# Attention layer of a two-layer decoder step on one core: sample pairs and prompt heads in one written-out program

## The chip, the core and the metric

The kernel runs on one core of a Trainium2 chip. The core has five engines with an instruction queue each: TensorE (PE: matmuls and transposes into PSUM), VectorE (DVE), ScalarE (ACT), GpSimd (POOL) and SyncE (SP, which here issues DMA transfers). They run side by side and meet through semaphores only; each works through its queue in order, so that an instruction that waits holds up all that stands behind it on its engine. PSUM has eight banks of 128 partitions by 512 numbers of 32 bits.

The metric is the device time of one execution in microseconds (us), as the median of several runs.

## What is computed

One inference step of a decoder with two layers, for a prompt of 256 tokens and for 8 samples of 4 new tokens each (32 rows) with 256 cached positions. Layer 0 is a gated delta-rule mixer and a mixture of experts, layer 1 is differential attention and a mixture of experts. The change is in layer 1's attention:

```python
def diff_attention(q, k, v, q_pos, k_pos, lam):
    ...
    s = jnp.einsum('bqhcd,bkhcd->bhcqk', qblk, k).astype(F32)
    mask = k_pos[None, :] <= pblk[:, None]
    p = jax.nn.softmax(jnp.where(mask, s, -jnp.inf), axis=-1)
    a = p[:, :, 0] - lam * p[:, :, 1]
    return jnp.einsum('bhqk,bkhe->bqhe', a.astype(v.dtype), v)
...
def diff_mixer(xn, k_rows, v_rows, q_pos, k_pos, w_q, lam_p, subln, w_out, lam_init):
    q = (xn @ w_q).reshape(B, L, DIFF_HEADS, 2, DIFF_DH)
    q = rope(q, q_pos) * (DIFF_DH ** -0.5)
    ...
    o = diff_attention(q, k, v_rows, q_pos, k_pos, lam)
    o = rms_norm(o, subln) * (1.0 - lam_init)
    return o.reshape(B, L, D_MODEL).astype(xn.dtype) @ w_out
```

There are 8 heads of two halves of 64. Keys and values of the new tokens come from one projection (`w_kv`, 1024 to 2048) and are outputs too; those of the past lie in a cache of pages of 128 rows, two pages for each sample, found through `page_table`. All is in float32.

## The kernel before

The program is five phases that follow each other with a barrier between: `gdn_phase`, `moe_phase` (layer 0), `attn_phase`, `moe_phase` (layer 1), `final_phase`. Weights pass through nine slots in SBUF, `slots` 0 to 8, 2 MB each. An expert phase works in groups of two experts, six slots to a group (gate, up and down matrices of two experts), and its SyncE queue fills each slot again when it is free. `m["prefetch"]` fills slots for the phase that comes. In the attention phase slots 0 to 5 hold the projection weights first; then slots 0 and 1 (`flat[0]`) hold the cached keys `Kc` and values `Vc` of two samples, slot 2 the spread queries `QB`, slots 4 and 5 the output weights `w_out`. Slots 6 to 8 share memory with the phase's own tiles.

`attn_phase` writes out one queue for each engine. On TensorE the order is:

1. **Projections.** For each half of 512 columns: keys, values and queries of the two prompt tiles (8 matmuls a tile, L1618), then all three for the 32 sample rows in one bank (`few`, L1626). DVE rotates keys and queries by position (`rotate`, L1467 to L1472), ACT scales the values into `v_t`. After the second half PE waits for all rotations, and transposes the sample rows (L1635).
2. **Samples** (`samples(pair)`), a loop over four pairs of samples. PE turns the cached keys, 32 transposes in eight groups of four over the four banks `B[4]` to `B[7]` (L1655), which DVE and ACT copy into `XK` (L1499, L1369). Then come the scores (L1666), a softmax over DVE and ACT (L1503 to L1510, L1371) in which PE runs 12 filler matmuls (`keep_busy`, L1642), the turned weights (L1672 to L1674), the sum over values (L1684), and transposes of the result (L1690), which DVE copies into `oT` (L1525). After the loop the sample rows are normed: a sum by a matmul with ones (L1697), a root on ACT, a reciprocal and a product on DVE (L1538, L1539).
3. **Heads** (`heads(i, ...)`), four rounds of two prompt heads, u = 0 and 1. PE makes the scores (L1721), turns queries and keys of the next two heads (L1709, from slices that GpSimd cut out, L1331), and runs 16 fillers. DVE adds the mask and finds maxima (L1548 to L1551), ACT takes four exponentials a head (L1392), DVE makes the weights (L1556 to L1565), PE turns them (L1734), ACT copies (L1399), PE multiplies by the values (L1745 to L1747), ACT squares and copies (L1405, L1406).
4. **Output.** Root, reciprocal and scaling of the prompt rows (L1415, L1585, L1588), transposes (L1759), the output projection of the prompt rows (64 records, L1766) and of the sample rows (L1770), and adds to the residual.

P, the sample's scores, and Pu, the heads' scores, are one tile; so are the sample's and the heads' maxima and sums. SyncE loads all keys of a pair when the keys of the pair before are turned, and its values when the pair's values are used. The output weights and expert piece 3 are issued ahead of the second pair's keys:

```python
            sp.wait_ge(s["kv_made"], 14)
            sp.dma_start(w_out, m["w_out_b"][0].rearrange("(h p) n -> p h n", p=128)).then_inc(s["wout_in"], 16)
            m["prefetch"](sp, 1, (3,))
            with sp.Fori(1, PAIRS) as pair:
                cache(0, pair, True)
                cache(1, pair, True)
```

## Time and profile before

| | us |
|---|---|
| median of 3 runs | 1624.23 |
| lowest and highest | 1622.6, 1625.52 |
| the profiled execution | 1618.63 |
| its span, first to last instruction | 1616.8 |
| attention phase on PE, from 847 to the next phase's start at 1126.8 | 280 |
| expert phase of layer 1 and the final norm, from there to the end | 490 |

The profile is of one execution. An engine is busy while it runs an instruction; the time of a PE instruction is counted to its modelled end, so that neighbours overlap. "Clock" is the share of TensorE's full speed (2.4 GHz) that was granted; 0.50 is 1.2 GHz. Each time in the trace is from the start of the span.

### The profile page before, as it was taken

The page shows a single profiled execution, that of the slowest core. Times are in us where ns is not written, and L with a number is a line of the kernel's source. Part 1 is how long each engine was busy: PE and PEld are TensorE (multiplying, and loading weights), DVE is VectorE, ACT ScalarE, POOL GpSimd, SP SyncE. Part 2 cuts the span into 40 slices and gives each one's busy share as a digit, 9 for nine tenths or more (in the row PEclk, how much of TensorE's full clock was granted, in tenths as well). Part 3 has the DMA queues.
Part 4 walks back from the last instruction along what each step waited for, and adds up shares of the span by engine and source line. Part 5 has one row for each costly group of instructions (what it writes and reads, how often), then busy time and mean ns, then how long its engine had stood idle before and what let it go on. Part 6 is the DMA issues. An engine that isn't in the chain of part 4 may idle for free. (4 is left out here: it accounts for less than half of the span.)

```text
span 1616.8 us, 21249 instructions
## 1 busy us (share of the span) xinstructions
PE 1514.0 (94%) x7887; PEld 772.9 (48%) x7887; DVE 641.2 (40%) x1656; ACT 299.2 (19%) x755; POOL 83.1 (5%) x143
## 2 busy tenths in 40 slices
PE   9999999999999999989989987869999999999986
PEld 8787877666333333333334444564633333333332
DVE  2656564545324242322333233551523333332324
ACT  2524243213101010000011011361210001010001
POOL 0101010101000000000000000100000000000000
PEclk9999999999999999999999989989999999999998
DMA  6432321639999999999993257504799999999994
GB/s 218 129 109 70 111 70 69 235 110 357 425 426 426 426 426 427 427 426 427 426 392 155 104 189 286 212 1 190 307 425 426 426 426 426 427 426 428 425 425 150
DMA packets 121838, 484.52 MB, mean 300 GB/s; under 512 B 18314, under 2 KB 53038, under 8 KB 73634
## 3 DMA queue, kind: packets, MB, share of 16 engines
q1 hardware_dynamic: 117442, 479.05, 73.6%
q0 software_dynamic: 4320, 4.42, 0.8%
q8 instruction: 53, 0.87, 0.2%
q14 instruction: 23, 0.19, 0.0%
HBM read 483.77 MB, written 10.97 MB: 306 GB/s over the span
## 5 line engine op out<-in xcount | busy, mean ns | idle before, releaser
L2360 PE MATMUL moe_ps_gate<-slots,moe_xrT 128*64 128x512 f32 x1024 | 229.0, 596 | 19.9 <-DMA slots<-in_w_gate_e_dram 19.9
L2360 PE MATMUL moe_ps_up<-slots,moe_xrT 128*64 128x512 f32 x1024 | 226.8, 595 | 0.0
L2388 PE MATMUL moe_ps_y<-slots,router_inputs 128*64 128x512 f32 x960 | 212.6, 595 | 0.0
L2240 DVE TENSOR_TENSOR resid<-resid,moe_ps_x 128x512 f32<-128x512 f32 x60 | 41.3, 688 | 265.2 <-PE moe_ps_x L2404 265.2
L2360 PEld LDWEIGHTS moe_ps_gate<-slots,moe_xrT 128*64 128x64 f32 x1024 | 73.6, 137 | 149.0 <-issue 148.0
L2360 PEld LDWEIGHTS moe_ps_up<-slots,moe_xrT 128*64 128x64 f32 x1024 | 71.3, 137 | 150.8 <-issue 138.7
L907 PE MATMUL gdn_bank<-gdn_xT,slots 128*128 128x288 f32 x512 | 133.0, 409 | 0.7 <-ACT slots L455 0.7
L2388 PEld LDWEIGHTS moe_ps_y<-slots,router_inputs 128*64 128x64 f32 x960 | 66.4, 137 | 124.8 <-issue 124.6
L2031 ACT ACTIVATE moe_xrT<-moe_ps_x,router_inputs 128x128 f32<-128x128 f32 x128 | 36.6, 369 | 379.5 <-PE moe_ps_x L2348 363.9
L907 PEld LDWEIGHTS gdn_bank<-gdn_xT,slots 128*128 128x128 f32 x512 | 93.9, 190 | 24.8 <-issue 1.8
L2209 DVE TENSOR_TENSOR router_inputs<-router_inputs,moe_ps_up 128x512 f32<-128x512 f32 x32 | 22.0, 689 | 195.3 <-PE moe_ps_up L2360 195.3
L2037 ACT ACTIVATE router_inputs<-moe_ps_gate 128x512 f32<-128x512 f32 x32 | 19.1, 598 | 233.3 <-PE moe_ps_gate L2360 233.3
L2404 PE MATMUL moe_ps_x<-moe_y_sb,router_inputs 128*128 128x512 f32 x120 | 59.5, 618 | 0.0
L1995 POOL DMA_INDIRECT moe_xrT<-xn_rows,moe_rows_in x30 | 31.0, 1032 | 526.4 <-PE moe_ps_x L2348 524.5
L2047 ACT COPY moe_y_sb<-moe_ps_y 128x512 f32<-128x512 f32 x32 | 18.8, 587 | 193.4 <-PE moe_ps_y L2388 176.5
L2232 DVE COPY moe_y_sb<-moe_ps_y 128x512 f32<-128x512 f32 x30 | 20.7, 692 | 81.3 <-PE moe_ps_y L2388 81.3
L2224 DVE TENSOR_SCALAR moe_place<-consts,moe_lpos,moe_gcur 128x128 f32<-128x128 f32 x192 | 52.1, 345 | 1.2
L2244 DVE TENSOR_TENSOR resid<-resid,moe_ps_up 32x256 f32<-32x256 f32 x112 | 46.2, 413 | 2.6
L1618 PE MATMUL at_bank<-slots,at_XK 128*128 128x512 f32 x96 | 41.7, 594 | 0.0
L1618 PE MATMUL at_pair<-slots,at_XK 128*128 128x512 f32 x96 | 41.5, 592 | 0.0
L665 DVE SCALAR_TENSOR_TENSOR slots<-slots,gdn_cw 128x312 f32<-128x312 f32 x72 | 39.2, 545 | 2.5
L2404 PEld LDWEIGHTS moe_ps_x<-moe_y_sb,router_inputs 128*128 128x128 f32 x120 | 20.3, 189 | 38.7 <-issue 38.7
(508 smaller groups left out, 1909.9 us busy)
## 6 DMA issues: line engine op xcount, KB each, us to landing
slots<-in_w_gate_e_dram SPq DMA_DIRECT2D x128, 1024.0 KB, 26.1
slots<-in_w_up_e_dram SPq DMA_DIRECT2D x128, 1024.0 KB, 26.5
slots<-in_w_down_e_dram SPq DMA_DIRECT2D x128, 1024.0 KB, 26.4
slots<-in_w_in_a_dram SPq DMA_DIRECT2D x16, 1024.0 KB, 5.5
slots<-in_w_kv_dram SPq DMA_DIRECT2D x4, 2048.0 KB, 17.1
slots<-in_cache_k_dram SPq DMA_DIRECT2D x16, 512.0 KB, 5.0
slots<-in_cache_v_dram SPq DMA_DIRECT2D x16, 512.0 KB, 5.5
slots<-in_state_delta_dram SPq DMA_DIRECT2D x8, 512.0 KB, 7.3
```

Of the source, the lines that this page charges most:

```text
L665: ins = V.scalar_tensor_tensor(acc[:, a, j, 0:ACC_COLS], src, cw[:, a, j, tap:tap + 1], acc[:, a, j, 0:ACC_COLS], ALU.mult, ALU.add)
L907: last = T.matmul(PB[i % 2][:, 0:T_ALL], w4[:, j, k, 128 * a:128 * a + 128], xT[:, k, :], start=(k == 0), stop=(k == KT - 1))
L1618: last = T.matmul(bank[:, :], XK[:, 0 if j < 2 else 1, k, at[t]], wslot[3 * half + j][:, k, :], start=(k == 0), stop=(k == KT - 1))
L1995: pool.indirect_dma_start(xg, None, xn_dram[:, :], bass.IndirectOffsetOnAxis(rows_in[:, :], 0), bounds_check=T_ALL - 1, oob_is_err=False). ...
L2031: last = A.activation(xgT[:, k, :], ps_x[:, 1, k - 4, :], ACT.Copy, scale=norm_T[:, k:k + 1])
L2209: V.tensor_tensor(hid, hid, ps_up[:], ALU.mult).then_inc(s["hidden"], 1)
L2224: last = V.tensor_scalar(place[:, k, t, :], m["lanes"][:, :], where[:, k, t:t + 1], gcur[:, k, t:t + 1], ALU.is_equal, ALU.mult)
L2240: V.tensor_tensor(half, half, banks[i][:, :], ALU.add).then_inc(s["summed"], 1)
L2244: V.tensor_tensor(part, part, banks[i][32 * q:32 * q + 32, 0:256], ALU.add).then_inc(s["summed"], 1)
L2360: last = T.matmul(ps[64 * e:64 * e + 64, :], xgT[:, k, 64 * e:64 * e + 64], slots[:, slot[2 * n + e], 512 * k:512 * k + 512], start=(k == ...
L2388: last = T.matmul(ps_y[64 * e:64 * e + 64, h, :], hidT[:, k, 64 * e:64 * e + 64], slots[:, slot[4 + e], 1024 * k + 512 * h:1024 * k + 512 ...
L2404: last = T.matmul(banks[i][:, :], selT[:, at[t]], y_sb[:, 512 * h:512 * h + 512], start=True, stop=True)
```

## The change

All of it is in `attn_phase`; the other phases are the same.

- Steps 2 and 3 become one program of four steps, written out without loops. Step i does sample pair i and heads 2i and 2i + 1, and turns keys for pair i + 1 and queries and keys for the next two heads in between.
- PSUM: turned keys have two banks (`turned_keys`, B[4] and B[5]) and not four, one copied by DVE and one by ACT. All small products of a pair share `S_bank` (B[6]), the sums over values of the pair and of both heads share `V_bank` (B[7]). Heads use the bank pairs `BB[u]` throughout.
- The sample's scores, weights, maxima and sums get tiles of their own (`sP`, `saT`, `smx`, `ssm`).
- Heads are transposed straight from `q_t` and `k_t`, sample scores read `QB` straight; GpSimd's copies go.
- Projections of the second half run in the order keys, sample rows, queries, (transposes of the sample rows), values.
- Keys are loaded a sample at a time, each when its place has been turned. The first loads of the second pair stand ahead of the output weights, and expert piece 3 stands behind all cache loads.
- Fillers: 8 and 8 in the last step, none in the others.
- The norm of the sample rows comes behind the last step, and their output projection ahead of the prompt rows' transposes.

The core of the diff, on PE and SyncE:

```diff
-            kbanks, vbanks, qbanks, few = (B[5], B[6]), (B[7], B[0]), (B[1], B[2]), B[3]
+            kbanks, vbanks, qbanks, few = (B[5], B[6]), (B[7], B[2]), (B[1], B[0]), B[3]
+            turned_keys, S_bank, V_bank = (B[4], B[5]), B[6], B[7]
+            out_banks = (B[5], B[7], B[6], B[0])
...
+            keys(0, 0)
+            keys(0, 1)
+            values(0)
+            sp.wait_ge(s["rotated"], 6)
+            rows_out(0)
+            for b in range(2):
+                sp.wait_ge(s["KT_made"], 4 * b + 4)
+                keys(1, b)
+            sp.wait_ge(s["kv_kept"], 6)
+            rows_out(1)
             sp.wait_ge(s["kv_made"], 14)
             sp.dma_start(w_out, m["w_out_b"][0].rearrange("(h p) n -> p h n", p=128)).then_inc(s["wout_in"], 16)
+            for pair in range(1, STEPS):
+                if pair < STEPS - 1:
+                    sp.wait_ge(s["KT_made"], 8 * pair + 4)
+                    keys(pair + 1, 0)
+                sp.wait_ge(s["od_made"], pair)
+                values(pair)
+                if pair < STEPS - 1:
+                    sp.wait_ge(s["KT_made"], 8 * pair + 8)
+                    keys(pair + 1, 1)
             m["prefetch"](sp, 1, (3,))
-            with sp.Fori(1, PAIRS) as pair:
-                cache(0, pair, True)
-                cache(1, pair, True)
...
+            for j in range(3):
+                project(0, j)
+            project_samples(0)
+            project(1, 0)
+            project_samples(1)
+            project(1, 2)
+            pe.wait_ge(s["rotated"], 6)
+            pe.wait_ge(s["q_rotated"], 4)
...
+            project(1, 1)
...
+            for i in range(STEPS):
+                more = i < STEPS - 1
+                sample_scores(i)
+                for u in range(2):
+                    scores(i, u)
+                if more:
+                    for j in range(2):
+                        turn_keys(i + 1, 0, j)
+                else:
+                    keep_busy(B[5], 0, 8)
+                sample_turned(i)
+                if more:
+                    for j in range(2, 4):
+                        turn_keys(i + 1, 0, j)
+                    for u in range(2):
+                        turn(i + 1, u)
+                else:
+                    keep_busy(B[5], 0, 8)
+                sample_values(i)
+                for u in range(2):
+                    weights_turned(i, u)
+                if more:
+                    for j in range(2):
+                        turn_keys(i + 1, 1, j)
+                sample_out(i)
+                if more:
+                    for j in range(2, 4):
+                        turn_keys(i + 1, 1, j)
+                for u in range(2):
+                    head_out(i, u)
+
             pe.wait_ge(s["od_sq"], 1)
-            T.matmul(B[0][:, 0:256], ones[:, :], rot2[:, 0:256], start=True, stop=True).then_inc(s["od_sum"], 1)
...
+            T.matmul(S_bank[:, 0:256], ones[:, :], rot2[:, 0:256], start=True, stop=True).then_inc(s["od_sum"], 1)
+            pe.wait_ge(s["od_done"], 1)
+            pe.wait_ge(s["wout_in"], 16)
```

The same steps in VectorE's queue:

```diff
+            for i in range(STEPS):
+                more = i < STEPS - 1
+                sample_scores(i)
+                scores(i, 0)
+                sample_weights(i)
+                if more:
+                    keys_kept(i + 1, 0, 0)
+                scores(i, 1)
+                sample_turned(i)
+                if more:
+                    keys_kept(i + 1, 0, 2)
                 for u in range(2):
                     weights(i, u)
+                sample_rows(i)
+                if more:
+                    keys_kept(i + 1, 1, 0)
+                sample_out(i)
+                if more:
+                    keys_kept(i + 1, 1, 2)
```

PE's queue in the second round of the sample loop, before. The names are tiles: `slots` holds the cached keys, `at_P` the scores and `at_aT` the weights.

```order
L1655 MATMUL at_bank<-consts,slots 128x128 x16
L1652 REGISTER_ALU
L1655 MATMUL at_bank<-consts,slots 128x128 x16
L1658 REGISTER_ALU
L1661 REGISTER_ALU
L1666 MATMUL at_pair<-at_XK,at_QBs 32x288 x16
L1642 MATMUL at_pair<-consts 128x128 x12
L1672 MATMUL at_pair<-consts,at_P 128x64
L1673 MATMUL at_pair<-consts,at_P 128x64
L1674 MATMUL at_pair<-consts,at_P 32x64
L1675 ISA
L1684 MATMUL at_pair<-slots,at_aT 32x512 x8
```

The same engine from the sample scores of a step to its sample values, now:

```order
L1708 MATMUL at_bank<-at_XK,slots 32x288 x16
L1760 MATMUL at_pair<-at_qkT 128x128 x2
L1760 MATMUL at_pair<-at_qkT 128x256 x2
L1760 MATMUL at_pair<-at_qkT 128x128 x2
L1760 MATMUL at_pair<-at_qkT 128x256 x2
L1692 MATMUL at_bank<-consts,slots 128x128 x8
L1715 MATMUL at_bank<-consts,at_sP 128x64
L1716 MATMUL at_bank<-consts,at_sP 128x64
L1717 MATMUL at_bank<-consts,at_sP 32x64
L1692 MATMUL at_bank<-consts,slots 128x128 x8
L1748 MATMUL at_pair<-consts,at_q 128x128 x2
L1748 MATMUL at_pair<-consts,at_k 128x128 x2
```

The 12 fillers (L1642) between scores and turned weights have given way to the scores of two heads and eight key transposes, which stood in one block of 32 ahead of the scores.

VectorE's queue before, in a round of the heads:

```order
L1548 TENSOR_TENSOR at_P<-at_pair,consts 128x768
L1549 TENSOR_REDUCE at_mx<-at_P 128x2
L1550 TENSOR_REDUCE at_mx<-at_P 128x2
L1551 TENSOR_SCALAR at_mx<-at_mx 128x4
L1548 TENSOR_TENSOR at_P<-at_pair,consts 128x768
L1549 TENSOR_REDUCE at_mx<-at_P 128x2
```

And now, from the scores of head 0 to those of head 1 of a step:

```order
L1565 TENSOR_TENSOR at_P<-at_pair,consts 128x768
L1566 TENSOR_REDUCE at_mx<-at_P 128x2
L1567 TENSOR_REDUCE at_mx<-at_P 128x2
L1568 TENSOR_SCALAR at_mx<-at_mx 128x4
L1531 RECIPROCAL at_ssm<-at_ssm 128x1
L1532 TENSOR_TENSOR at_ssm<-at_ssm,at_coef 128x1
L1533 TENSOR_SCALAR at_sP<-at_sP,at_ssm 128x288
L1516 COPY at_XK<-at_bank 128x2x256
L1565 TENSOR_TENSOR at_P<-at_pair,consts 128x768
```

The sample's weights and a copy of turned keys stand between the two heads' scores.

## Rows read from the trace of the kernel before

**Rows 1.** Stages: stretch, length, busy us (instructions), clock, DMA, GB/s.

```profile
847.00:946.90 99.90, 99.79 (x312) 42.86 (x312) 29.39 (x82) 9.97 (x15) 1.81 (x1) 1.00 0.30 112
946.90:963.10 16.20, 9.26 (x48) 8.33 (x48) 8.68 (x32) 3.95 (x8) 0.61 (x1) 0.58 0.81 288
963.10:1031.40 68.30, 51.39 (x456) 33.39 (x456) 22.70 (x69) 10.85 (x22) 3.26 (x7) 0.95 0.74 271
1031.40:1083.80 52.40, 40.75 (x298) 35.46 (x298) 33.56 (x90) 31.08 (x126) 4.33 (x12) 0.89 0.21 88
1083.80:1126.80 43.00, 35.00 (x145) 17.36 (x145) 7.02 (x11) 5.21 (x11) 0.01 (x1) 0.90 0.36 147
1126.80:1616.80 490.00, 465.57 (x2234) 183.47 (x2234) 174.17 (x432) 60.44 (x134) 21.67 (x34) 0.98 0.94 392
```

**Rows 2.** Timeline of PE, projections to scores: start, us, what, idle before.

```profile
951.53 1.06 PE L1635 MATMUL at_bank<-consts,at_q 32*128 32x32 f32 x8 [4.63 <-DVE at_q L1472]
...
963.16 2.15 PE L1666 MATMUL at_pair<-at_XK,at_QBs 128*32 128x288 f32 x32 [0.68 <-ACT at_XK L1369]
```

**Rows 3.** Timeline of PE, second and third sample pair.

```profile
979.30 3.67 PE L1655 MATMUL at_bank<-consts,slots 128*128 128x128 f32 x16 [5.31 <-DMA slots<-in_cache_k_dram]
...
1000.08 1.97 PE L1655 MATMUL at_bank<-consts,slots 128*128 128x128 f32 x16 [0.68 <-ACT at_XK L1369]
...
1002.80 2.15 PE L1666 MATMUL at_pair<-at_XK,at_QBs 128*32 128x288 f32 x32 [0.75 <-ACT at_XK L1369]
...
1009.37 1.92 PE L1684 MATMUL at_pair<-slots,at_aT 128*32 128x512 f32 x16 [0.50 <-DVE at_aT L1515]
...
1013.18 0.65 PE L1690 MATMUL at_pair<-consts,at_rot 128*128 128x128 f32 x4 [0.90 <-DVE at_rot L1517]
```

**Rows 4.** DVE: timeline of a pair and a heads round; last, lines by form.

```profile
1005.01 0.42 DVE L1503 COPY at_P<-at_pair 128x256 f32<-128x256 f32 x1 [2.67 <-PE at_pair L1666]
...
1007.16 0.17 DVE L1508 RECIPROCAL at_sm<-at_sm 128x1 f32<-128x1 f32 x1 [0.70 <-ACT at_P L1371]
...
1007.56 0.37 DVE L1510 TENSOR_SCALAR at_P<-at_P,at_sm 128x288 f32<-128x288 f32 x1
...
1062.27 0.96 DVE L1548 TENSOR_TENSOR at_P<-at_pair,consts 128x768 f32<-128x768 f32 x1
...
1064.42 0.18 DVE L1556 RECIPROCAL at_sm<-at_sm 128x4 f32<-128x4 f32 x1
...
L1499 DVE COPY at_XK<-at_bank 128x512 f32<-128x512 f32 x10 | 6.7, 690 | 4.7 <-PE at_bank L1655 4.7
```

**Rows 5.** Timeline of PE, head rounds.

```profile
1066.38 0.55 PE L1734 MATMUL at_bank<-consts,at_P 128*128 128x128 f32 x3 [1.21 <-DVE at_P L1565]
...
1081.37 0.39 PE L1745 MATMUL at_bank<-at_v,at_aT 128*128 128x128 f32 x2
```

**Rows 6.** Timeline of PE in the output part; last, of DVE.

```profile
1087.96 3.67 PE L1759 MATMUL at_pair<-consts,at_q 128*128 128x128 f32 x16 [4.21 <-DVE at_q L1588]
...
1092.41 27.73 PE L1766 MATMUL at_bank<-slots,at_oT 128*128 128x512 f32 x64 [0.78 <-ACT at_oT L1419]
...
1120.08 3.66 PE L1770 MATMUL at_pair<-slots,at_oT 128*32 128x256 f32 x64
...
1033.18 1.75 DVE L1538 RECIPROCAL at_rot<-at_rot 128x256 f32<-128x256 f32 x1 [1.82 <-ACT at_rot L1377]
```

**Rows 7.** Stretches as in rows 1, shorter.

```profile
979.70:983.00 3.30, 3.27 (x16) 2.86 (x14) 1.38 (x2) 0.59 (x1) 0.00 (x0) 0.50 0.90 369
995.30:1011.70 16.40, 13.37 (x130) 8.83 (x122) 6.25 (x18) 2.98 (x6) 0.61 (x1) 1.00 0.72 256
1041.00:1044.50 3.50, 1.17 (x9) 0.93 (x10) 2.57 (x10) 2.36 (x10) 0.00 (x0) 1.00 0.33 138
1044.80:1047.50 2.70, 2.70 (x16) 2.48 (x16) 0.00 (x0) 1.71 (x11) 0.00 (x0) 0.50 0.00 0
1108.50:1126.70 18.20, 15.24 (x92) 6.82 (x90) 3.03 (x6) 0.00 (x0) 0.00 (x0) 0.99 0.02 10
```

478 lines of the change are left out of this document (227 added, 251 removed).

## The prediction

> **What bounds the kernel now.** I read the table of stages first, then the row of TensorE (PE) through the attention layer, then what VectorE (DVE) and ScalarE (ACT) do while PE waits, then the granted clock. Stages [rows 1]: the second expert layer, from 1126.8 us to the end, keeps the DMA engines busy 94% of the time, since it streams all expert weights. The attention layer ahead of it is not bound by DMA. Its projections (847 to 946.9 us) are solid PE work. Then come 16.2 us of getting started (PE busy 9.3), 68.3 us in which the four sample pairs run one after another, 52.4 us in which the eight prompt heads run two at a time, and 43.0 us of output projection. In the two middle stages PE, DVE and ACT take turns: in the heads stage DVE has 33.6 and ACT 31.1 us of work in 52.4 us, and part of what PE does there is filler. So these 121 us are a chain of hand-offs. What shortens it moves the start of the expert layer, and that layer's first six-slot group is already loaded or loaded at its start, so the rest should move with it one to one: the stream of weights restarts when the layer starts.
>
> **The change, part by part.** I walk the new program against PE's row.
>
> *From projections to the first sample scores.* Before, PE ends projecting at 946.9 us, stands 4.63 us for the last rotation, transposes the sample rows (1.06 us and as much again for the keys), and begins the first sample scores at 963.16 us [rows 2]: 16.3 us. Now the sample rows of the second half are projected ahead of the query and value tiles, so their rotation and the transposes (about 2 us) lie in the projections. What is left behind the last projection is 8 groups of four key transposes and two head turns. Sixteen key transposes took 1.97 us at full clock [rows 3], so a group is 0.5 us. A head turn, four transposes of the same shape, is 0.5 too. That is 5 us. Since turned keys now have two PSUM banks and not four, a group waits for the copy of the group two ahead of it: a copy takes 0.69 us on DVE [rows 4], the group 0.5, so three or four times PE stands some 0.35 us. Sum 6.3 us, with the 2 us moved inward 8.4. Gain 16.3 - 8.4 = 7.9 us. It counts on the clock: before, the stage had 0.58 of full speed after the 4.63 us wait [rows 1, 2], and that wait is gone.
>
> *One step (a pair and two heads).* I set t = 0 at the start of the sample scores. They take 2.1 us on PE [rows 3]; the scores of the two heads and two key groups follow on PE to 4.7. DVE then has the long chain. Sample scores to maximum: from 1005.01 to the reciprocal at 1007.16, less the exponential of 0.70 between them, 1.45 us, so to 3.5. Scores of head 0: 1062.27 to 1064.42, 2.15, to 5.7. Sample weights: from 1007.16 to the end of the scaling at 1007.93, 0.8, to 6.5. Key copy 0.7, to 7.2. Scores of head 1 to 9.4. Copies of the turned sample weights 0.5 (PE's wait for them at 1009.37 [rows 3]), to 9.9. Key copy to 10.6. Weights of heads 0 and 1, 1.96 each (1064.42 to the PE row it releases at 1066.38), to 14.5 [all rows 4, 5]. PE then has the turn of the second head's weights 0.55 [rows 5], two key groups 1.0, the sample output transposes 0.65 [rows 3], two key groups 1.0, and the head outputs: six matmuls, whose first takes 0.39 with its drain [rows 5] and whose others follow at the fillers' pace or a little faster, 1.3. The next scores begin at **19.1 us**. The sample value matmuls (some 3 us on PE from 1009.37 [rows 3]) and the sample's exponential and the ACT copies lie beside that chain. PE waits about 1.9 us once (4.7 to 6.6, for the sample weights) and 1.2 us once (for head 1's weights), elsewhere under half a microsecond. The last step has no keys to turn: DVE ends its weights at 13.1, PE its head outputs at 15.8. Four steps: 3 x 19.05 + 15.8 = 73.0 us. Before, from 963.16 to the end of the last head output at 1083.7, 120.6 us. Gain 47.6 us. In it is the 5.31 us that PE stood for the keys of the second pair [rows 3], which were queued behind the output weights (4 MB) and an expert piece (2 MB). Now both halves of these keys are queued ahead of the output weights, and the expert piece behind all cache loads. What is late next are the third pair's keys and the second pair's values, behind those 4 MB; by the walk they are wanted some 4 us after they should land. If they are late, it costs at most the same 5.3 us once.
>
> *The tail.* Before, PE stands 4.21 us after the last head output (root, reciprocal, scaling), transposes for 3.67 us at half clock, and starts the output projection at 1092.41 [rows 6]. Now the sample rows' norm, which used to lie between pairs and heads, comes here, and PE waits for it first: its reciprocal alone is 1.75 us [rows 6], so PE stands about 6.0 us. The sample rows' projection (3.66 us [rows 6]) then runs ahead of the transposes; after such a wait it starts at 1.2 GHz as the transposes did, so I take 5.5. It hides the scaling, and the transposes run at full clock, 2.0. The large projection starts 13.6 us after the last head output, against 8.7 before, and is no longer followed by the 3.66 us. Between the end of PE's last matmuls (1120.08 + 3.66) and the layer's start at 1126.8 lie 3.1 us with four adds; now it is one, and I take 1 us for the other three. Sum: +4.9 - 3.7 - 1 = +0.2, call it **0.3 us lost**.
>
> *What costs nothing.* GpSimd's copies of queries and of head slices go; they lay beside PE work. Loops written out: their branches and register sums go, some tenths of a microsecond in each round, which I don't count. Expert pieces 3, 0, 2, 1 and the router inputs are issued before the tail, more than 40 us ahead of the layer's start. Pieces 6 to 8 were issued at the start of the output projection, and at 1108.5 DMA stood still [rows 7]: 16 us, and now they have 28. If that cover were gone, the expert layer would start with a wait for them.
>
> *The clock.* The walk is at full clock. The filler matmuls are gone, except for 16 in the last step. In the heads stage PE ran 1.17 us of 3.5 (1041 to 1044.5) and the clock was then 0.50 for 2.7 us; such falls came in three of four rounds and before the transposes. In the sample rounds, with waits under 1 us, it stayed at 1.00 [rows 7]. A step's 1.9 us wait lies between the two. From below the cost is 0; from above, a fall in each step and one of them twice as long, 2.7 us or more of half speed, so 1.4 to 2 us each, up to 9 in all. I take one short fall per step, 1.4 x 4 = 5.5 us, since one wait and its neighbours leave PE busier than that heads row.
>
> A rule bears on this: the Trainium skill, TensorE: Matmul & The Clock Gate, Part 4: PE-mode transpose, says that transposes do not count as work for the clock. By it the new filling of the waits, key and head transposes, would be worth nothing to the clock. Rows 7 speak against it: between 979.7 and 983.0 PE ran key transposes alone at 0.50, and that was enough: the rounds behind it ran at 1.00.
>
> **Sum.** 7.9 + 47.6 - 0.3 - 5.5 = 49.7 us. The profiled execution was 1618.6 us (span 1616.8 and 1.8 around it), 5.6 under the median of 1624.2. So 1569 for its like, and **1574 us** for the median.
>
> **Rivals.**
> 1. *The interleaving holds less than walked.* DVE and ACT are in order, so one late hand-off delays the other stream too. For it: DVE carries 15 us of each 19, with two chains through ACT. Against it: each queue is written in the order in which I find the results. Before, a pair and a heads round took 16.4 + 12.4 = 28.8 us. If half of what I claim of it is lost, a step is 24 us, 4 x 4.9 = 20 us back: 1594; a quarter gives 1584.
> 2. *The clock stays at 1.2 GHz through all steps*, by the transpose rule or because no filler is left. PE has some 15.5 us of work in a step: 13.4 in a pair's 16.4 us [rows 7], less 12 fillers of 0.24 us (as two key transposes [rows 3]), and 5 for two heads (1.1 and 1.3 [rows 5], 1.0 for the turns, 1.6 for the scores, estimated from the same shapes). At half speed that is 31 us, so 12 us more in three steps and 10 in the last: 46 us, in place of 5.5: 1615. The rule cited above would give this time.
> 3. *Slower: it stays there through the tail as well.* The output projection is 27.7 us of solid matmuls [rows 6] and doubles, with 4 for the rest: 1615 + 31 = 1646. It decides when more than 110 us run at half speed, as each such microsecond costs half of one. Against it: before, 3.67 us of transposes at half clock were enough, and the 64 output matmuls behind them took 0.43 us each from the first on [rows 6].
> 4. *The change does not bring the end forward*, since the expert layer gives the gain back. For it: its DMA share of 0.94. Against it: DMA stood at about zero from 1108.5 to 1126.7 [rows 7], so it isn't the stream that was late when the layer began. Time 1620 to 1625.
>
> **Numbers.** Forecast (1564 to 1581, with the bounds 0 and 9 us for the clock and the 5.3 of late loads) 0.70; rival 1, 1581 to 1594, 0.18; rival 2 0.04; rival 3 0.03; rival 4 0.05. The range 1562 to 1590 takes in the forecast and most of rival 1. A measurement here can tell about 0.2% (3 us) from no change. Faster by more: 0.70 + 0.18 + 0.04 = 0.92; same 0.04; slower 0.04 (rival 3 and the far side of rival 4).
>
> **What the new profile would show.** Right: no PE wait over 1 us between the last projection and the first sample scores, scores of the pairs 19 to 21 us apart, no wait on the key or value cache, a PE wait near 6 us before the sample rows' projection, and the same 490 us from the expert layer's start to the end. Wrong if pairs lie 24 us or more apart (then see which engine PE waits for), if the clock row shows 0.5 over whole steps, or if the expert layer takes longer than 490 us.

## The result and the profile after

The changed kernel takes 1559.74 us (median of 4 runs, 1558.21 to 1562.42), against 1623.6 for the kernel before in the same comparison (4 runs, 1622.6 to 1625.52). The ratio is 0.9615, 95% interval 0.9589 to 0.9641: 64 us less. The forecast was 1574 us in a range of 1562 to 1590. The direction was right, and the time lies 14 us below the forecast and 2 us below the range.

The profiled execution of the changed kernel took 1558.21 us, its span 1556.4. First its stages, to be laid beside [rows 1] (stretch, length, then busy us and instructions of PE, PEld, DVE, ACT, POOL, the granted clock, DMA share, GB/s):

```profile
846.70:949.40 102.70, 102.70 (x328) 45.31 (x329) 35.68 (x110) 10.86 (x18) 1.81 (x1) 0.98 0.32 120
949.40:955.70 6.30, 5.13 (x43) 4.28 (x42) 2.77 (x4) 4.14 (x9) 0.00 (x0) 1.00 0.24 69
955.70:1025.10 69.40, 63.16 (x552) 43.52 (x553) 50.94 (x157) 35.54 (x134) 0.00 (x0) 0.93 0.80 290
1025.10:1068.10 43.00, 35.55 (x149) 16.54 (x148) 9.17 (x14) 6.06 (x17) 0.05 (x1) 0.96 0.70 288
1068.10:1556.40 488.30, 466.86 (x2234) 183.37 (x2234) 174.23 (x432) 60.40 (x134) 21.62 (x34) 0.98 0.94 393
```

The sample pairs and the prompt heads took 68.3 and 52.4 us one after the other. Together they now take 69.4, with PE busy 91% of it. That is 51 of the 60 us by which the profiled span is shorter. PE's row through these four steps:

```profile
955.69 2.15 PE L1708 MATMUL at_bank<-at_XK,slots 128*32 128x288 f32 x32 [0.72 <-DVE at_XK L1516]
...
962.04 0.43 PE L1715 MATMUL at_bank<-consts,at_sP 128*128 128x64 f32 x2 [1.66 <-DVE at_sP L1533]
...
973.76 2.15 PE L1708 MATMUL at_bank<-at_XK,slots 128*32 128x288 f32 x32
...
979.41 1.62 PE L1692 MATMUL at_bank<-consts,slots 128*128 128x128 f32 x8 [1.99 <-DMA slots<-in_cache_k_dram]
...
991.87 2.15 PE L1708 MATMUL at_bank<-at_XK,slots 128*32 128x288 f32 x32
...
1005.82 0.88 PE L1768 MATMUL at_pair<-consts,at_P 128*128 128x128 f32 x6
...
1010.35 2.15 PE L1708 MATMUL at_bank<-at_XK,slots 128*32 128x288 f32 x32
...
1025.13 0.60 PE L1824 MATMUL at_bank<-at_rot,consts 128*128 128x256 f32 x2
...
1031.16 5.25 PE L1829 MATMUL at_bank<-slots,at_oT 128*32 128x256 f32 x64 [5.43 <-DVE at_oT L1612]
```

The rows of 2.15 us are the sample scores, where a step begins. The first begins at 955.69 (955.3 by the walk, at 963.16 in [rows 2]), the next three 18.07, 18.11 and 18.48 us apart, and the last step is 14.78 long. The walk had 19.05 and 15.8. In each of the first three steps PE stands once for 1.6 to 2.0 us (in the second it is for the third pair's keys), and in the last for 0.62. The last row is the samples' projection, behind the longest wait of the tail.

The granted clock fell to 0.50 once in each of the first three steps, for about 3 us. The prediction had charged one such fall in each of the four. One of these falls, and the one behind the tail's wait:

```profile
1000.50:1003.50 3.00, 3.00 (x17) 1.88 (x19) 2.86 (x13) 2.68 (x11) 0.00 (x0) 0.50 0.01 3
1031.20:1034.60 3.40, 3.40 (x36) 1.64 (x40) 2.43 (x3) 0.00 (x0) 0.00 (x0) 0.53 1.01 429
```

And DVE's row in the third step. It has no gap from 994.09 to 1005.36:

```profile
994.09 0.42 DVE L1523 COPY at_sP<-at_bank 128x256 f32<-128x256 f32 x1 [3.19 <-PE at_bank L1708]
994.43 0.18 DVE L1524 TENSOR_TENSOR at_sP<-at_bank,consts 128x32 f32<-128x32 f32 x1
...
995.21 0.96 DVE L1565 TENSOR_TENSOR at_P<-at_pair,consts 128x768 f32<-128x768 f32 x1
...
997.99 0.68 DVE L1516 COPY at_XK<-at_bank 128x512 f32<-128x512 f32 x1
998.59 0.95 DVE L1565 TENSOR_TENSOR at_P<-at_pair,consts 128x768 f32<-128x768 f32 x1
...
1001.63 0.15 DVE L1573 RECIPROCAL at_sm<-at_sm 128x4 f32<-128x4 f32 x1
...
1003.45 0.17 DVE L1573 RECIPROCAL at_sm<-at_sm 128x4 f32<-128x4 f32 x1
...
1004.61 0.75 DVE L1582 SCALAR_TENSOR_TENSOR at_P<-at_P,at_sm 128x128 f32<-128x128 f32 x2
1005.96 0.69 DVE L1546 COPY at_rot<-at_bank 128x512 f32<-128x512 f32 x1 [0.60 <-PE at_bank L1731]
```

PE turns the heads' weights from 1005.82 on. DVE had them ready at 1005.36 (1004.61 and 0.75). So two chains end this step within half a microsecond of each other: DVE's, and PE's own work, which had the clock fall in it. That is the question for the experiments.

### The profile page after: what moved, and what is told of

Same layout as the page of the kernel before. It is cut to its first block and busy times, and to the rows that moved or that the text cites. A ratio compares the mean times of both kernels' runs of the same rounds, so it can differ in the third digit from the quotient of the medians.

```text
span 1556.4 us, 20606 instructions
## 1 busy us (share of the span) xinstructions
PE 1485.6 (95%) x7695; PEld 744.9 (48%) x7695; DVE 638.5 (41%) x1656; ACT 294.5 (19%) x753; POOL 74.6 (5%) x123
```

## Experiments: what the parts are worth

Each kernel was compared with the kernel before on the same chip. The chips differ by a few microseconds, so between comparisons the ratios are set side by side, and small effects are read from the traces. "Steps" is the time from the first sample scores to the last head output: 69.4 us in the changed kernel.

**The loops written out, nothing else** (nine loops of this kind):

```
-            with sp.Fori(1, PAIRS) as pair:
+            for pair in range(1, PAIRS):
```

> The kernel before, with nothing changed but that the attention stages' nine register loops are written out for every step. Theory (order of the work is what pays): the written-out form alone gives 0 to 2 us of the 64, 1622 to 1624 us. Rival (the loops' registers, branches and semaphore arithmetic held the engines up): 10 us or more, under 1614 us.

Measured: 1618.43 us against 1619.38, ratio 0.9998 (0.9982 to 1.0013). Writing out the program is worth nothing by itself, within the 2 to 3 us that this comparison can tell. It is only what makes another order possible.

**The new layout, the old order of the work.** The four pairs run first, then the heads:

(PE's part; the other engines' orders follow it, SyncE loads a pair's values ahead of the next pair's keys, and twelve and sixteen fillers stand in PE's waits as before.)

```
+            for i in range(STEPS):
+                sample_scores(i)
+                keep_busy(B[0], 0, 12)
+                sample_turned(i)
+                sample_values(i)
+                sample_out(i)
+                if i < STEPS - 1:
+                    for b in range(2):
+                        for j in range(4):
+                            turn_keys(i + 1, b, j)
+            for u in range(2):
+                turn(0, u)
             for i in range(STEPS):
                 more = i < STEPS - 1
-                sample_scores(i)
                 for u in range(2):
                     scores(i, u)
...
```

> The changed kernel with its PSUM layout, its projection order and its written-out program, but the four sample pairs one after the other first and the prompt heads behind them, as in the kernel before. Theory (interleaving fills the waits of one chain with the work of the other): the 47.6 us of the step-by-step part come back, 1600 to 1612 us. Rival (the new layout of PSUM and of the key loads carries a good part by itself): under 1590 us.

Measured: 1613.39 us, ratio 0.9969 (0.9951 to 0.9987). The two stretches of its trace, and its one long wait for a load:

```profile
953.30:1016.70 63.40, 49.80 (x458) 32.73 (x459) 21.33 (x64) 9.53 (x20) 0.00 (x0) 1.00 0.86 313
1016.70:1069.40 52.70, 38.85 (x296) 34.73 (x295) 31.57 (x93) 27.84 (x118) 0.00 (x0) 0.90 0.29 118
...
978.72 1.92 PE L1721 MATMUL at_bank<-slots,at_saT 128*32 128x512 f32 x16 [2.72 <-DMA slots<-in_cache_v_dram]
```

They sum to 116.1 us, against 120.6 before and 69.4 when interleaved. By the traces the interleaving is worth 46.7 us and the layout, with its key loads, 4.5; up to 2.7 of the 46.7 is this wait for the second pair's values, which neither the kernel before nor the changed one has. The first theory holds. The median lies 1 us above the bound expected. By the ratios the interleaving would be worth more, some 55 us: the profiled execution (1606.6) was the fastest of ten, and where the others lose another 7 us no trace shows.

**The old order of the projections.**

```
             project(1, 0)
-            project_samples(1)
+            project(1, 1)
             project(1, 2)
+            project_samples(1)
...
             last.then_inc(s["dT_made"], 1)
-            project(1, 1)
```

> The changed kernel with the second half's projections in the old order (keys, values, queries, then the samples' rows), so that the samples' rotation and transposes come after them all. Theory (the projection order took the wait ahead of the first step): 5 to 8 us slower than the changed kernel, 1565 to 1568 us. Rival (the wait went by the layout, not by the order): 1559 to 1561 us.

Measured: 1566.63 us, ratio 0.9685 (0.9669 to 0.9702), where the changed kernel has 0.9615, and 0.9628 and 0.9626 in two later comparisons: 9 to 11 us, more than the 5 to 8 expected. PE stands for the rotation again, as in [rows 2], and then for the copies of the turned keys:

```profile
954.00 1.03 PE L1677 MATMUL at_bank<-consts,at_q 32*128 32x32 f32 x8 [4.72 <-DVE at_q L1481]
...
956.90 1.97 PE L1692 MATMUL at_bank<-consts,slots 128*128 128x128 f32 x8 [1.01 <-ACT at_XK L1353]
...
964.73 2.15 PE L1708 MATMUL at_bank<-at_XK,slots 128*32 128x288 f32 x32 [0.72 <-DVE at_XK L1516]
```

The start of the whole phase wanders with the layer before, and the clock is at 0.50 for up to 6 us there in some executions. So the distance is taken from the phase's first matmuls, at 846.64 here, to the first sample scores, at 964.73: 118.1 us. Eight of the other traces with the changed order of projections had as long a fall at that place (a mean clock of 0.72 over the phase's first 12 us, as here), and all of them have 110.2 to 110.3. So the order is worth 7.8 us at the same clock, and the prediction's 7.9 for this part stands, with its cause.

**The old order of the loads.** The output weights and one expert piece stand ahead of the second pair's keys on SP's queue:

```
-            for b in range(2):
-                sp.wait_ge(s["KT_made"], 4 * b + 4)
-                keys(1, b)
...
             sp.dma_start(w_out, m["w_out_b"][0].rearrange("(h p) n -> p h n", p=128)).then_inc(s["wout_in"], 16)
+            m["prefetch"](sp, 1, (3,))
+            for b in range(2):
+                sp.wait_ge(s["KT_made"], 4 * b + 4)
+                keys(1, b)
...
                     keys(pair + 1, 1)
-            m["prefetch"](sp, 1, (3,))
```

> The changed kernel with the output projection's weights and one piece of the expert weights queued ahead of the second pair's keys, as before. Theory (SP's queue serves in order, so the second pair's keys would arrive behind 4 to 6 MB): the second step waits 8 to 14 us for its keys and some of that is lost, 1564 to 1574 us. Rival (the loads only change places, the transfers being the bound of the whole stretch anyway, and the time is given back in the expert layer): 1559 to 1561 us.

Measured: 1573.48 us, ratio 0.9733 (0.9716 to 0.9751). The first step takes 32.35 us instead of 18.1, by one wait, which the expectation had at 8 to 14 us and in the second step. The rival falls: the expert layer gives back no more than about 1 us of it (487.1 against 488.3).

```profile
976.35 1.97 PE L1692 MATMUL at_bank<-consts,slots 128*128 128x128 f32 x8 [15.83 <-DMA slots<-in_cache_k_dram]
```

The same order cost the kernel before only 5.31 us [rows 3]. The keys did not come later here: their matmuls start at 976.35, against 979.30 before. But PE comes to them at 960.52, behind the first scores, where it came at 973.99, behind a whole sample pair. It is 13.5 us earlier and the keys only 3.0, which makes 15.83 of 5.31. A faster chain needs its loads sooner: in the new program a load order left as it was would have taken back a quarter of the gain by the trace (14.3 us), and somewhat more by the ratios. The prediction had set 5.3 us as the most that late loads can cost; for the order it judged that stood, but as a general bound it would have been wrong by three times. So the parts measured here (46.7, 4.5, 7.8 and 14.3) add up to 73 us and not to 64: they overlap, as the layout's 4.5 us has a change of the loads in it, and what a load order is worth depends on the order of the work.

## Experiments: what ends a step

**Two more VectorE copies in its chain.**

```
+                for _ in range(2):
+                    link(V.tensor_copy(rot2[:, 0:384], m["causal"][:, :]))
                 for u in range(2):
                     weights(i, u)
```

> The changed kernel with two further VectorE copies (128x384, results unused) in each of the four steps, ahead of the heads' weights. In the trace of the changed kernel VectorE runs without a gap from 994.09 to 1005.36 in the third step. Theory (VectorE's chain ends the step, TensorE is just behind it): each copy takes 0.5 to 0.6 us, so 1.0 to 1.2 us a step less 0.4 us of slack, +2 to +5 us over the changed kernel, 1562 to 1565 us. Rival (TensorE's own work is the path, VectorE has slack): 0, 1559 to 1560 us.

Measured: 1562.25 us, ratio 0.9642 (0.9615 to 0.9668). The ratio is 4 us above the changed kernel's, within what was expected, but the intervals overlap; the steps take 71.2 us in all, 1.8 more. Its first three steps, and PE's wait for the heads' weights in each:

```profile
956.59:975.18 18.59, 15.31 (x140) 10.19 (x140) 13.97 (x42) 8.51 (x28) 0.00 (x0) 1.00 0.99 381
975.18:993.71 18.53, 15.39 (x142) 10.10 (x141) 13.90 (x42) 10.18 (x38) 0.00 (x0) 1.00 0.94 346
993.71:1012.24 18.53, 16.64 (x142) 11.46 (x141) 13.91 (x42) 10.19 (x38) 0.00 (x0) 0.91 0.45 153
...
970.99 0.55 PE L1770 MATMUL at_pair<-consts,at_P 128*128 128x128 f32 x3 [1.28 <-DVE at_P L1582]
...
989.52 0.55 PE L1770 MATMUL at_pair<-consts,at_P 128*128 128x128 f32 x3 [1.20 <-DVE at_P L1582]
...
1008.05 0.55 PE L1770 MATMUL at_pair<-consts,at_P 128*128 128x128 f32 x3 [0.31 <-DVE at_P L1582]
```

Here is the plainest line of the study: the third step had a clock fall (0.91, PE busy 1.25 us longer), the second none, and both took 18.53 us. With DVE's chain longer, PE stands 1.28 and 1.20 us for the heads' weights in the steps without a fall and 0.31 in the one with it. The fall eats a wait and costs nothing.

**Fillers in PE's wait.**

```
                     for j in range(2):
                         turn_keys(i + 1, 0, j)
+                    keep_busy(V_bank, 384, 6)
```

(In the second step, where PE waits for keys, the fillers stand ahead of the key turns. They write into the bank of the value sums, so PE's wait for that bank moves ahead of them.)

> The changed kernel with six 128x128 filler matmuls (results unused) in TensorE's wait of each of the first three steps, so that its granted clock doesn't fall to 0.50 behind it. Theory (VectorE's chain ends at 1005.36, where TensorE comes at 1005.82, so the fall is all but hidden): -0.5 to -1.5 us against the changed kernel, 1558 to 1559 us. Rival (each fall costs the path its 1.4 us, as the prediction had it): -4 to -5 us, 1555 to 1556 us.

Measured: 1561.73 us, ratio 0.9648 (0.9622 to 0.9675). No fall is left in the steps (the clock is 1.00 throughout), and they are 17.82, 17.81 and 17.74 us apart: 68.2 us in all, 1.3 less than with three falls. That agrees with the theory. The median is 3 us over the one expected and shows no gain at all; where it went the section on the clock shows.

**Two key copies from DVE to ACT.** First DVE's program, then ACT's.

```
                 sample_weights(i)
-                if more:
-                    keys_kept(i + 1, 0, 0)
                 scores(i, 1)
                 sample_turned(i)
-                if more:
-                    keys_kept(i + 1, 0, 2)
...
                 sample_exp(i)
-                head_exp(i, 0)
                 if more:
+                    keys_kept(i + 1, 0, 0)
                     keys_kept(i + 1, 0, 1)
+                head_exp(i, 0)
+                if more:
+                    keys_kept(i + 1, 0, 2)
                 head_exp(i, 1)
```

> The changed kernel with the two key copies of VectorE that stand in its unbroken chain (one pair's first page halves, 0.6 us each) on ScalarE instead, in each of the first three steps. Theory A (VectorE's chain alone ends the step): -1.2 us a step, -3.6 us, 1556 us. Theory B (VectorE's chain and TensorE's, slowed by its clock fall, end within 0.5 us of each other): -0.5 to -1.5 us alone, 1558 to 1559 us.

**Both together.** The fillers and the copies.

> The changed kernel with both: the six fillers in TensorE's wait and the two key copies on ScalarE. Theory B (the two chains end within 0.5 us of each other, so that only both edits together shorten the step): -3 to -5 us, 1555 to 1557 us, more than the sum of the two alone. Theory A (VectorE's chain alone ends the step): no more than the copies alone give. Clock rival: no more than the fillers alone give.

Measured: 1556.98 us (ratio 0.961, 0.9585 to 0.9635) and 1555.78 us (0.9603, 0.958 to 0.9627). First the version with the copies alone, first and second step:

```profile
956.17:974.16 17.99, 16.33 (x140) 11.68 (x140) 12.23 (x38) 9.50 (x30) 0.00 (x0) 0.91 1.01 390
974.16:990.83 16.67, 14.90 (x142) 10.15 (x141) 12.07 (x38) 11.17 (x40) 0.00 (x0) 1.00 0.97 358
```

And the first step of the version with both:

```profile
952.61:969.23 16.62, 16.30 (x153) 11.60 (x153) 12.06 (x38) 9.70 (x30) 0.00 (x0) 1.00 0.99 381
```

A step with a fall stays at 17.99, the same step without one takes 16.62: the fall costs 1.4 us as soon as DVE's chain is out of its way. That is the price the prediction had worked out for it. In the first step, with its fall, theory B holds: the copies alone bring 0.1 us. In the second and third no fall came in this execution, and they take 16.67 and 16.55, which is 1.1 and 1.2 us less than a step without a fall (17.74): the two copies' 0.6 each, within a tenth or so. So neither theory holds for all executions: which chain ends a step is decided by whether the clock falls in it.

In the version with both, the second step took 18.80 us. PE stood 1.28 us for keys there and 1.36 more ahead of the value matmuls, for which the trace names no releaser:

```profile
975.70 1.09 PE L1691 MATMUL at_bank<-consts,slots 128*128 128x128 f32 x8 [1.28 <-DMA slots<-in_cache_k_dram]
...
980.67 1.92 PE L1730 MATMUL at_bank<-slots,at_saT 128*32 128x512 f32 x16 [1.36 <-issue]
```

Its steps sum to 66.9 us, against 66.2 with the copies alone, so "more than the sum of the two alone" is shown for the first step only. The next edit moves the loads, and the version with all edits tests whether they ended this step.

**The output weights loaded two steps later.**

```
-            sp.wait_ge(s["kv_made"], 14)
-            sp.dma_start(w_out, m["w_out_b"][0].rearrange("(h p) n -> p h n", p=128)).then_inc(s["wout_in"], 16)
...
                     keys(pair + 1, 1)
+                if pair == 1:
+                    sp.wait_ge(s["kv_made"], 14)
+                    sp.dma_start(w_out, m["w_out_b"][0].rearrange("(h p) n -> p h n", p=128)).then_inc(s["wout_in"], 16)
```

> The changed kernel with the output projection's weights (4.2 MB) queued two steps later, behind the third pair's keys, which come late in the second step (TensorE waits 1.99 us for them). Theory (the wait is covered by VectorE's chain): -0.5 to 0.5 us, the steps stay at 18.1. Rival (the wait is on the path): the second step 1 to 2 us shorter, -1 to -2 us over all.

> The changed kernel itself, as the reference for the other three on the same chip: 1556 to 1562 us.

Measured on one chip: 1562.73 us (ratio 0.9634, 0.9611 to 0.9658) beside the changed kernel's 1562.07 (0.9628, 0.9605 to 0.9652). The wait for keys (0.97 us beside it) is gone, and the second step takes 17.73 us where it had 17.91. By itself it is worth nothing that a median shows, as expected: DVE's chain covers the wait.

## Experiments: the tail and the clock

**The tail in another order.**

```
-            pe.wait_ge(s["od_done"], 1)
-            pe.wait_ge(s["wout_in"], 16)
-            for h in range(H):
-                for g in range(4):
-                    last = T.matmul(B[4][32 * g:32 * g + 32, 0:256], oT[:, h, at[2]], w_out[:, h, 256 * g:256 * g + 256], start=(h == 0), stop=(h == H - 1),
-                                    tile_position=(0, 32 * g))
-            last.then_inc(s["out_made"], 1)
+            keep_busy(B[5], 0, 12)
```

These matmuls stand between the projections of the first and the second prompt tile now. ScalarE and VectorE take the prompt rows' norm ahead of the samples'.

> The changed kernel with the tail in another order: the prompt rows are normed and turned first, twelve filler matmuls (results unused) stand in TensorE's wait, and the samples' rows are projected between the two prompt tiles. Theory (the 5.43 us wait for the samples' norm and the clock fall behind it, 0.50 from 1031 to 1034, are both on the path): the stretch from the last head to the expert layer's first transposes goes from 42.9 to 38 to 40.5 us, 1555 to 1557 us. Rival (the prompt rows' own norm and copies become the wait, since they stand on the same two engines): under 1 us gained.

Measured: 1556.85 us, ratio 0.9603 (0.9579 to 0.9626), beside 1562.07 for the changed kernel. From the last head output to the expert layer's first transposes it takes 40.74 us, against 42.93 and 42.87 in two traces of the changed kernel. The theory had 38 to 40.5. PE stands 1.89 us there instead of 5.43, and the samples' projection takes 3.66:

```profile
1031.08 2.23 PE L1831 MATMUL at_pair<-consts,at_q 128*128 128x128 f32 x16 [1.89 <-DVE at_q L1616]
1033.18 13.97 PE L1845 MATMUL at_bank<-slots,at_oT 128*128 128x512 f32 x32
1047.09 3.66 PE L1839 MATMUL at_bank<-slots,at_oT 128*32 128x256 f32 x64
```

**All four edits.**

> The changed kernel with all four edits: six fillers in TensorE's wait of each step, two key copies on ScalarE, the output projection's weights two steps later, the tail in the other order. In the version with the fillers and the copies the first and third step took 16.6 and 16.5 us, and the second 18.8, with 1.28 and 1.36 us of waits for keys and values. Theory (these late loads are what then ends the second step): all three at 16.5 to 16.8 us, the tail at 38 to 40.5 us, -7 to -9 us over all, 1549 to 1552 us. Rival (the transfers' sum, not their order, sets the second step): it stays over 18 us, 1552 to 1555 us.

Measured: 1555.23 us, ratio 0.9579 (0.9556 to 0.9602): faster than the changed kernel on the same chip by 6.8 us in the medians. The steps are 16.61, 16.92, 16.82 and 14.97 us, 65.3 in all: the late loads were what ended the second step, and the rival (the transfers' sum) falls. The median missed the 1549 to 1552 expected by 3 us: the second step is a little over its 16.8, and the tail took 42.3 us and not 38 to 40.5, since the clock fell in it.

**No fall anywhere**, and two further combined versions, with the changed kernel beside them on one chip. The first has the six fillers of each step and, in the tail:

```
             pe.wait_ge(s["od_sq"], 1)
             T.matmul(S_bank[:, 0:256], ones[:, :], rot2[:, 0:256], start=True, stop=True).then_inc(s["od_sum"], 1)
+            keep_busy(B[5], 0, 20)
             pe.wait_ge(s["od_done"], 1)
```

> The changed kernel itself, as the reference for the other three on the same chip: 1556 to 1563 us.

> The changed kernel with six filler matmuls in TensorE's wait of the first three steps and twenty in its wait in the tail (results unused, 4.8 us in a wait of 5.43), so that the granted clock stays at 1.00 in both. Theory (the falls in the steps are hidden behind VectorE, the one in the tail is paid by the samples' projection, 5.25 us where 3.66 were measured at 1.00): -1.3 us in the steps, -1.6 us in the tail, -2 to -3.5 us over all. Rival (each fall is paid, as the prediction had it): -4.1 us in the steps by three falls and -1.6 in the tail, -5 to -6 us.

> The combined version with nineteen filler matmuls instead of twelve in the tail, 4.5 us against a gap of 4.7. In the combined version the tail took 42.3 us, with the clock at 0.50 from 1029 to 1032, and 40.7 without that fall in the version with the tail's edit alone. Theory (TensorE's 1.89 us of wait behind the fillers lets the clock fall): no fall, the tail 39.5 to 41 us, -9 to -11 us against the changed kernel. Rival (the clock falls all the same, after the long stretch without a fall): the tail stays over 42 us, -7 us.

> As the version before (two key copies on ScalarE, output weights loaded later, the tail's other order with nineteen fillers) but without the fillers in the steps. Theory (with VectorE's chain 1.2 us shorter the clock falls are no longer covered by it): one or two of the first three steps at 17.5 to 18 us instead of 16.6 to 16.9, 1 to 2.5 us slower than with them. Rival (the fillers do nothing): the same time.

Measured: 1561.0 us (ratio 0.9626, 0.9609 to 0.9644) for the changed kernel, 1553.03 (0.9592, 0.9577 to 0.9606) without falls, 1553.66 (0.9594, 0.9581 to 0.9607) and 1554.13 (0.9613, 0.9589 to 0.9636) for the two combined versions. The steps and the tail by the traces (us):

| | steps, first to last | sum | tail |
|---|---|---|---|
| changed kernel, three falls in the steps | 18.07, 18.11, 18.48, 14.78 | 69.4 | 42.9 |
| the same, one fall (the run beside these) | 18.02, 17.73, 17.74, 14.78 | 68.3 | 43.4 |
| no falls | 17.81, 17.74, 17.74, 14.78 | 68.1 | 41.4 |
| all edits, 19 fillers in the tail | 16.61, 16.92, 17.21, 14.97 | 65.7 | 40.8 |
| the same without the steps' fillers | 17.99, 16.54, 17.16, 14.97 | 66.7 | 40.7 |

In the steps of the changed kernel a fall costs 0.2 to 0.7 us while DVE's chain covers it, and it cost 1.4 in the first step of the last version. In the tail nothing covers it: the samples' projection takes 3.66 us at full clock, 5.25 and 5.77 after the wait. The combined version's tail had no fall and took 40.8, as its theory said, but its medians gained 7 us and not 9 to 11. Without the steps' fillers the steps take 1.0 us more, the least of what was expected. In the third step of the last version PE stood 1.05 us for the fourth pair's keys, and in the one before it 1.19 at the same place with no releaser named; it is probably the price of loading the output weights ahead of these keys. So in both stretches the theory holds, with 2.3 us between the kernel without falls and its neighbour.

But the medians are 8 us apart, which neither theory said. The traces show where: from the start of the expert layer's row on, the changed kernel's run took 493.1 us and the one without falls 488.0.

The first 3.5 us of the expert layer and the next 10.5, of the changed kernel in this comparison:

```profile
1067.20:1070.70 3.50, 3.49 (x23) 3.17 (x23) 2.73 (x6) 3.33 (x7) 2.56 (x3) 0.65 0.70 208
1070.70:1081.20 10.50, 10.50 (x56) 10.07 (x55) 1.49 (x9) 7.80 (x5) 0.71 (x1) 0.50 0.99 393
```

The same of the changed kernel in its first profile:

```profile
1068.10:1071.60 3.50, 3.50 (x19) 3.17 (x20) 2.48 (x6) 3.38 (x7) 2.51 (x3) 0.57 0.75 215
1071.60:1082.10 10.50, 10.50 (x98) 10.26 (x98) 5.36 (x24) 7.67 (x5) 0.96 (x1) 0.98 0.99 383
```

And of the combined version with 19 fillers in the tail:

```profile
1063.80:1067.30 3.50, 3.45 (x28) 3.32 (x29) 2.85 (x8) 3.29 (x7) 2.56 (x3) 1.00 0.71 208
1067.30:1077.80 10.50, 10.50 (x100) 10.30 (x99) 5.69 (x29) 7.92 (x7) 0.96 (x1) 1.00 0.99 384
```

In the first the clock stays at 0.50 and PE gets through 56 instructions, in the others 98 and 100 in the same time. The three layers then take 493.1, 488.3 and 486.7 us. The other traces fall on the same three levels: 486.3 to 487.1 without a fall at its start (five kernels), 488.0 to 490.0 with one of about 3 us (the kernel before among them), 492.1 to 493.4 with a long one. The version with fillers in the steps alone, which gained 1.3 us in the steps and nothing in its median, had 493.4 in its profiled run. Which level comes changes from run to run of one kernel (488.3, 488.5 and 493.1 in three profiles of the changed one). All five traces with fillers in the tail had the low or the middle level, and four of the ten interleaved ones without had the high one. That is a hint that fillers in the tail keep the long fall away, and no proof.

But the level does not come by chance alone. In these ten traces PE waits the same 5.43 us in the tail, and the samples' projection behind that wait (3.66 us at full clock) takes longer the longer the fall lasts. Sorted by it, the levels fall into three groups:

| samples' projection in the tail | expert layer to the end |
|---|---|
| 5.00, 5.06, 5.19, 5.25 | 488.8, 488.4, 488.5, 488.3 |
| 5.77, 5.80, 5.81, 6.12 | 493.1, 493.0, 493.1, 493.4 |
| 6.41, 6.49 | 486.6, 487.1 |

So the fall at the layer's start goes with the fall in the tail ahead of it, and the two longest falls in the tail come with the shortest layers. That also speaks against the simple reading that any fall in the tail harms the layer. What ties the two together no run shows.

## Why the prediction was right, and where it was off

The mechanism was right: interleaving the two chains is what pays, and most of the gain came from there. The step that failed is the size of one term, the four steps: 78.5 us forecast, 69.4 measured. It rests on DVE's chain, walked too long, and on the clock's cost, laid on top of a walk that already had PE waiting. Of the signs named beforehand, one failed too: a wait on the key cache, 1.99 us, was not to be there.

**Start.** Gain 7.9 us forecast, 7.5 measured (963.16 to 955.69). Taking the sample rows' projection forward was the cause, as its own experiment shows with 7.8. The clock hides a part of the gain: the changed kernel's phase began with a fall (0.86 over its first 12 us). In the five traces of the changed front without one, the first scores come 107.4 us after the phase's start, against 116.05 before, which is 8.6 less.

**Steps.** Forecast 73.0 us at full clock and 78.5 with the falls; measured 69.4. This term was mis-sized by 9.1 us, in two places.

- *The walk was 4.9 us too long*: without falls the steps take 68.1, a step 17.74 where I had 19.05. PE's part was right to 0.2 us. The error is in DVE's chain: from the start of the sample scores' copy to the end of the heads' weights I had 12.4 us and it took 11.3. I had added up distances in a program where each link was followed by a wait, and busy times. In a chain without waits the next instruction starts before the end that the trace notes for the one before: the key copy has 0.68 us and its successor starts after 0.60; the sample scores' chain took 1.12 us where I had taken 1.45, the heads' weights 1.8 and 1.9 where I had 1.96 each, and the copies of the turned sample weights 0.34 where I had taken 0.5 from PE's wait for them. The Trainium skill, VectorE: DVE Perf Modes, Two Vector instructions with no wait between them, has a model for this: an instruction is held until all earlier ones have finished if its inputs or its output start in another group of 32 partitions than the last ones did, and one that is not held starts earlier. The rows agree as far as they go (0.60 us after the start of a copy of 0.68), since the operands of this chain all start at partition 0. No run here has operands that start elsewhere beside them, so the model itself is not tested.
- *The clock term was put on the wrong chain*: 5.5 us charged, 1.3 paid. I charged four falls, and three came; the price of one on PE's chain (1.4) was right. But I took the walk's end from DVE's chain, in which PE stands 1.9 and 1.2 us, and then added PE's loss on top of it. A loss on an engine that has waits in the step must be taken from these waits first. The experiment with more DVE work shows it with 18.53 us twice, and the one with less shows the full 1.4.

**Tail.** 0.3 us lost forecast, 0.1 gained measured. The wait was 5.43 us where I had 6.0, the samples' projection 5.25 where I had 5.5: here the fall is paid, and it was counted.

**Expert layer.** I had 490 us before and after; the profiles have 490.0 and 488.3. Both began with a fall of about 3 us, so both lie in the middle level (488.0 to 490.0), and what makes the 1.7 us between them stays open. By the levels above, any single profile can be 7 us off in this layer.

**From profile to median.** I added 5.6 us, since the profiled run before lay that much under its median. The profiled run after lies 1.5 under its own. In the other comparisons a profiled run lay between 6.8 under its median and 3.9 above it, so the 5.6 was the spread of runs and not a property of the kernel. With 9.1 for the steps, 1.7 for the layer, 0.4 for the tail, -0.4 for the start and about 3.5 for this (5.6 less 1.5, less what rounding 1574.5 to 1574 had taken off), the 14.3 us are accounted for.

**Rivals.** Interleaving that holds less: no, it held more. The clock at 1.2 GHz through all steps, and through the tail: no, although the rule on transposes from the Trainium skill, as the prediction cites it, would have it so. In the first step the clock rose while PE ran transposes alone (PE's row; the four rows of two are of one shape):

```profile
962.90 2.02 PE L1692 MATMUL at_bank<-consts,slots 128*128 128x128 f32 x8
964.71 0.64 PE L1748 MATMUL at_pair<-consts,at_q 128*128 128x128 f32 x2
...
965.56 0.63 PE L1748 MATMUL at_pair<-consts,at_q 128*128 128x128 f32 x2
965.99 0.47 PE L1748 MATMUL at_pair<-consts,at_k 128*128 128x128 f32 x2
```

The expert layer giving the gain back: no. The stream's share is 0.94 as before, and the layer started 59 us earlier and ended 60 us earlier. Late loads: the third pair's keys were late (1.99 us, hidden), and a load order that hadn't been changed would have cost 14 us.

**The range.** It left out the side on which I had charged something at its full price: with no clock cost at all the sum gives 1569, and the 7 us from there to the low end of 1562 were a margin with no term behind it, for a walk taken as exact. A walk built of hand-offs can be too long as well as too short, and here it was by 7%.

## What to carry to other kernels

When the walk of a new order has one engine in a gapless chain and another with waits, give every loss to its engine and let the waits absorb it before it is added to the sum. Interleave independent hand-off chains before anything else is tuned (46.7 us here, against nothing for writing out the loops), and move the loads forward with it, since a chain that runs faster meets its loads sooner. And when two versions differ by less than 5 us, compare the stretch that was edited in the traces, since a layer that nobody touched can be 7 us longer or shorter, and how the edited stretch ends can go along with that.

## What the runs showed of the hardware that was not expected

The same expert layer takes about 486.5, 488.5 or 493 us, by how the clock stands in its first 14 us, the same kernel shows more than one of these, and in ten traces the level went with the length of the fall in the tail ahead of it. A clock fall of about 3 us behind a wait of 1.6 us is not certain either: in the same place of the same program there were three in one profile and one or two in others, and six fillers (1.5 us of work) took them away in every one of the five kernels that had them. The price of a late key load is not a property of the load: the same queue order cost 5.31 us in the slower program and 15.83 in the faster, though the keys were there 3 us sooner.
